# Rotary embedding of two attentions: block copies and VectorE in place of TensorE permutation matmuls

## The reference

```python
def rope(x, pos):
    half = HEAD_DIM // 2
    inv = ROPE_THETA ** (-jnp.arange(half) / half)
    ang = pos[:, None] * inv[None, :]
    cos, sin = jnp.cos(ang)[None, :, None, :], jnp.sin(ang)[None, :, None, :]
    x1, x2 = x[..., :half], x[..., half:]
    return jnp.concatenate([x1 * cos - x2 * sin, x2 * cos + x1 * sin], axis=-1)

q = rope(q.reshape(b, s, N_HEADS, dh), pos)
ks = rope(ks.reshape(b, s, g_n, dh), pos)      # selected keys
kw = rope(kw.reshape(b, s, g_n, dh), pos)      # window keys
kc_c = compress(kc, cmp_pos[0], ...)           # blocks of 32 tokens + position bias, gelu MLP
```

## Time and profile before

| | |
|---|---|
| time, median of 3 runs | 1591.09 us (1590.78 to 1593.4) |
| the profiled execution's own time | 1591.71 us |
| its span, first to last instruction | 1589.9 us |
| TensorE busy | 1548.1 us, 97% |
| VectorE busy | 1179.4 us, 74% |
| ScalarE busy | 974.5 us, 61% |
| HBM read | 243.09 MB |
| granted TensorE clock, mean | 0.994 |

### The profile page before, as it was taken

How to read it: one execution, slowest core, us unless ns; L and a number is a source line. 1 busy time by engine, 2 the same in 40 slices (tenths; PEclk the granted TensorE clock), 3 DMA queues, 4 the chain that set the end, 5 groups by cost and what they waited for, 6 DMA issues and landing times.

```text
span 1589.9 us, 31250 instructions
## 1 busy us (share of the span) xinstructions
PE 1548.1 (97%) x13494; PEld 1460.2 (92%) x13494; DVE 1179.4 (74%) x1665; ACT 974.5 (61%) x1440; POOL 2.8 (0%) x10
## 2 busy tenths in 40 slices
PE   8999999999999999999999999989999998999998
PEld 7999999999989999999999887958999987799997
DVE  6899657777668799467777566866888677688864
ACT  7676864665547777665656451476777555677753
POOL 0000000000000000000000000000000000000000
PEclk9999999999999999999999999989999999999999
DMA  7523145555544321354655544501655543165551
GB/s 280 177 91 107 56 151 190 200 196 180 196 160 161 133 101 62 111 208 160 212 182 189 186 166 154 177 6 54 212 186 186 189 163 133 53 206 189 186 189 53
DMA packets 35849, 246.15 MB, mean 155 GB/s; under 512 B 4096, under 2 KB 4480, under 8 KB 6656
## 3 DMA queue, kind: packets, MB, share of 16 engines
q1 hardware_dynamic: 35712, 244.15, 44.5%
HBM read 243.09 MB, written 1.05 MB: 154 GB/s over the span
## 4 chain that ended last, share of the span: by engine, by line
PE 81%; DVE 12%; ACT 4%; DMA 1%; issue 1%; SPq 0%; DVEq 0%; ACTq 0%
PE PS L407 80%; DVE WL L1932 3%; DVE SB L1941 2%; DVE SB L1932 2%; ACT SB L1222 1%; ACT WH L1225 1%; DVE SA L1932 1%; DMA RAW<-w_in 1%; PE PS L410 1%; ACT SB L1225 1%; DVE SB L2200 1%; DVE SB L1936 0%; ACT SB L1798 0%; DVE SA L1941 0%; DVE SA L2102 0%
## 5 line engine op out<-in xcount | busy, mean ns | idle before, releaser
L407 PE MATMUL PS<-XH,WH 128*128 128x256 f32 (+1 forms) x2536 | 715.9, 282 | 11.5 <-DVE WL L1932 4.4
L407 PE MATMUL PS<-XL,WH 128*128 128x256 f32 (+1 forms) x2536 | 712.9, 281 | 0.0
L407 PE MATMUL PS<-XH,WL 128*128 128x256 f32 (+1 forms) x2536 | 712.6, 281 | 0.0
L1225 ACT CAST WH<-RAW 128x2048 fp32r<-128x2048 f32 (+1 forms) x229 | 427.0, 1865 | 369.9 <-PE PS L407 343.5
L1932 DVE TENSOR_TENSOR WL<-RAW,WH 128x2048 fp32r<-128x2048 f32 (+1 forms) x229 | 511.3, 2234 | 136.4 <-ACT WH L1225 132.3
L407 PEld LDWEIGHTS PS<-XH,WH 128*128 128x128 f32 (+1 forms) x2536 | 477.4, 188 | 18.6 <-issue 6.6
L407 PEld LDWEIGHTS PS<-XL,WH 128*128 128x128 f32 (+1 forms) x2536 | 475.4, 187 | 3.1 <-issue 2.4
L407 PEld LDWEIGHTS PS<-XH,WL 128*128 128x128 f32 (+1 forms) x2536 | 474.9, 187 | 0.4
L407 PE MATMUL PS<-INHL,WH 128*128 128x512 f32 (+1 forms) x1216 | 334.5, 344 | 1.2 <-DVE INHL L1932 1.2
L407 PE MATMUL PS<-INHL,WL 128*128 128x256 f32 x960 | 270.0, 281 | 0.0
L407 PEld LDWEIGHTS PS<-INHL,WH 128*128 128x128 f32 x1216 | 210.0, 188 | 29.2 <-ACT INHL L1225 1.5
(11 more groups left out here) (145 smaller groups left out, 1307.6 us busy)
## 6 DMA issues: line engine op xcount, KB each, us to landing
RAW<-w_in SPq DMA_DIRECT2D x51, 1024.0 KB, 4.9
RAW<-w_up SPq DMA_DIRECT2D x44, 1024.0 KB, 4.8
RAW<-f_in SPq DMA_DIRECT2D x44, 1024.0 KB, 4.9
RAW<-w_down SPq DMA_DIRECT2D x22, 1024.0 KB, 4.9
RAW<-f_out SPq DMA_DIRECT2D x22, 1024.0 KB, 4.8
RAW<-a_w_in SPq DMA_DIRECT2D x10, 1024.0 KB, 4.9
RAW<-w_out SPq DMA_DIRECT2D x8, 1024.0 KB, 4.8
RAW<-w_bdn SPq DMA_DIRECT2D x4, 1024.0 KB, 4.8
```

The lines of the kernel that those rows point to most:

```text
L407: return e.matmul(out, l, r, start=start, stop=stop, skip_group_check=True)
L1225: e.copy(out, x).then_inc(*A.up(*key, of=of))
```

## The change

TensorE no longer takes part in the rotation of queries and keys, nor in doubling the compressor's inputs.

- Queries: VectorE multiplies the projection from PSUM by the sines into `SN` and by the cosines into `RAWQ` (512 columns each). ScalarE copies `SN` to `TN` in four copies of 32 partitions, each block to its neighbour's place. VectorE subtracts `TN` from `RAWQ`. (Before, the sines' sign was that of the target half; taken at the source half, it calls for a subtraction.)
- Keys of the first attention: the same, two heads at a time; the result goes to one half of the partitions, and ScalarE copies it to the other half. Keys of the second attention: the same with 256 columns.
- Compressor: VectorE adds the bias to `kc_raw`, `vc_raw` in SBUF, and takes the source half's partitions for both target halves; the bias lies in a second, turned copy.
- `CD` and its two loads are gone. ScalarE's ten copies from PSUM to SBUF (`k_raw`, `q_raw`) are gone.
- The compressed keys are still rotated with `ROT`.
- Waits: scores wait for a whole query chunk and for both key projections.

```diff
+            def turned_halves(st, name, i, width=512):          # ScalarE
+                w.wait_ge(*V[name + " in", st, i])
+                if name == "q":
+                    waits(*([V["rope q", st, i - 2]] if i > 1 else [V["rope k", st, 0 if st == "s" else i]]))
+                for j in range(4):
+                    cp(TN[i % 2][QUART[j], 0:width], SN[i % 2][QUART[j ^ 1], 0:width], name + " turned", st, i)
...
+                def both_halves(n):
+                    w.wait_ge(*V["rope k", st, n])
+                    for h in range(2):
+                        cp(KKv[HALF[1 - h], h:4:2, n], KKv[HALF[h], h:4:2, n], "rope k", st, n)
...
-                k_raw(0)
-                k_raw(1)
+                chunk()
+                chunk()
                 hidden(0, 0)
                 hidden(0, 1)
+                turned_halves(st, "k", 0)
                 hidden(1, 0)
-                chunk()
+                turned_halves(st, "k", 1)
+                chunk()
+                both_halves(0)
                 hidden(1, 1)
+                both_halves(1)
                 tables("exp_and_others")
-                for c in range(4):
+                chunk()
+                w.wait_ge(*P["ps", st, "glT"])
+                act(gl, v3(ps[st, "glT"][:, 0:96], 2), ACT.Exp, "gl exp", scale=-1.0, of=ps.out(st, "glT"))
+                for c in range(3):
                     chunk()
-                    w.wait_ge(*P["ps", st, "q", c, 0])
-                    cp(RAWQ[:, c * 512:c * 512 + 512], ps[st, "q", c, 0][:, :], "q raw", st, c, of=ps.out(st, "q", c, 0))
+                    turned_halves(st, "q", c)
...
+                turned_halves(st, "q", 3)
                 for u in range(16 + 3):
...
+            def rope_in(st, name, i, x, out, cos, sin, of):     # VectorE
+                if name == "q":
+                    waits(*([A["q turned", st, i - 2], V["rope q", st, i - 2]] if i > 1 else
+                            [A["k turned", st, 0 if st == "s" else i]] if i == 0 or st == "n" else []))
+                n = x.shape[-1] // 256
+                x, sn = v3(x, n), v3(SN[i % 2][:, 0:256 * n], n)
+                tt(sn, x, sin.unsqueeze(1).to_broadcast([128, n, 256]), ALU.mult, name + " in", st, i, of=of)
+                tt(v3(out, n), x, cos.unsqueeze(1).to_broadcast([128, n, 256]), ALU.mult, name + " in", st, i, of=of)
+            def q_out(st, c):
+                s = slice(c * 512, c * 512 + 512)
+                waits(A["q turned", st, c], V["q in", st, c])
+                tt(Q[:, s], RAWQ[:, s], TN[c % 2], ALU.subtract, "rope q", st, c)
...
-                rope_q(st, 1)
-                chunk()
-                rope_q(st, 2)
+                q_out(st, 1)
+                chunk()
+                q_in(st, 2)
+                q_in(st, 3)
+                q_out(st, 2)
...
-                    if u == 1:
-                        rope_q(st, 3)
+                    if u == 0:
+                        q_out(st, 3)
...
                     if t_ < 3:                                  # second attention, VectorE's loop
-                        rope_q(st, t_ + 1)
+                        q_out(st, t_ + 1)
+                    if t_ < 2:
+                        q_in(st, t_ + 2)
```

More of the change, by code:

```diff
@@ L902, in ffn @@
                 down(st, nxt)
[L904 to L914, removed]
             def nsa():
                 st = "n"
[L919 to L926, removed]
                 def hidden(n, hf):
@@ L1041, in scores @@
                     wd, g = 128 * (j + 1), t_ // 2
-                    w.wait_ge(*V["rope q", st, t_])
-                    w.wait_ge(*V["rope k", 0, g])
-                    w.wait_ge(*V["rope k", 1, g])
+                    w.wait_ge(*V["rope q", st, t_ // 2])
+                    for n in range(2):
+                        w.wait_ge(*V["rope k", st, n])
+                        w.wait_ge(*A["rope k", st, n])
                     for r in range(2):
@@ L1893, in swa @@
                     if t_ < 2:
-                        q_raw(t_ + 2)
+                        chunk()
+                        turned_halves(st, "q", t_ + 2)
                     if t_ >= 3:
@@ L2605, in hidden_turn, with k_in, k_out @@
                        of=ps.out(st, "hidT", n))
-                def keys(n):
-                    for g in range(4):
-                        if n or g:
-                            w.wait_ge(*V["rope k", n if g else 0, g - 1 if g else 3])
-                        rope_k((st, "rope k", n, g), KK[:, g * 512 + n * 256:g * 512 + n * 256 + 256], g, "rope k", n, g)
+                def k_in(n):
+                    waits(P["ps", st, "k", n, 0], V["angles", st])
+                    rope_in(st, "k", n, ps[st, "k", n, 0][:, :], KU[n], COSr, SINr, ps.out(st, "k", n, 0))
+                def k_out(n):
+                    waits(A["k turned", st, n], V["k in", st, n])
+                    for h in range(2):
+                        tt(KKv[HALF[h], h:4:2, n], v3(KU[n], 2)[HALF[h]], v3(TN[n], 2)[HALF[h]], ALU.subtract, "rope k", st, n)
                 w.wait_ge(*V["angles", st])
@@ L2746, in swa @@
                 turn_rs(st, 1.0)
-                waits(V["angles", st])
-                for g in range(2):
-                    rope_k((st, "rope k", g), KK[:, g * 256:g * 256 + 256], g, "rope ks", g)
+                waits(V["angles", st], A["kv"])
+                rope_in(st, "k", 0, kv[:, 0:256], KU[0][:, 0:256], COSr, SINr, None)
+                waits(A["k turned", st, 0], V["k in", st, 0])
+                for h in range(2):
+                    tt(KK[HALF[h], h * 256:h * 256 + 256], KU[0][HALF[h], 0:256], TN[0][HALF[h], 0:256], ALU.subtract, "rope k", st, 0)
+                q_in(st, 0)
                 chunk()
-                w.wait_ge(*V["rope ks", 1])
-                rope_q(st, 0)
+                q_in(st, 1)
+                q_out(st, 0)
                 V.note("fs", st)
@@ L2944, in constants @@
     put("ROT", rot)
-    cd = np.concatenate([(s == (64 * g + (p % 64 + r) % 64)[None, :]) for r in (0, 32) for g in range(2)], axis=1)
     inv = f(10000.0) ** (-np.arange(32, dtype=f) / f(32))
```

126 lines of the change are left out of this document (44 added, 82 removed).

## The result

The kernel after takes 1595.58 us at the median (1592.57 to 1597.88) against 1592.88 us for the kernel before, timed beside it: ratio 1.0017, 95% interval 1.001 to 1.0025. It is slower by about 2.7 us where 16 us less were forecast. Its profiled execution took 1592.95 us, with a span of 1591.2 us and a mean granted clock of 0.990.

A forecast was written before the change was run, and what follows sets the result against it. TensorE was taken to bound the kernel; 12.7 us off the first attention (10.7 + 2.55 - 0.6) and 3.3 off the second made 16.0, so 1591.1 us would become 1575.1, range 1569.5 to 1582.

The forecast's parts named there:

- What bounds the kernel: Whole kernel: TensorE, busy 97% of the span; work taken off it is worth its time unless something else stands ready.
- (d): Rival, ScalarE's queue: exchanges delay the next weights' cast in 8 query chunks; at 1.7 us per copy, 1599 us; chance 0.03.
- (e): Rival: the first attention's late chains reach the loop and the saving is waited for; within 3 us of before; chance 0.05.
- TensorE: what goes: Both attentions: 44 plain f32 matmuls of 256 columns leave TensorE, 19.8 us of its work.
- Up to the query projections: First attention: compressor inputs 3.5 us, first keys' rotation 3.6 and 0.9 of the second keys' come off.
- The copies: ScalarE's exchange of halves: four 32x512 copies from SBUF to SBUF, 0.62 us each, 2.5 us.
- (b): Rival: copies between blocks of 32 partitions take 1.0 us each, costing 7 to 8 us, 1583 us; chance 0.09.
- (a): Rival: TensorE's clock falls in the new gaps, 1.7 us per fall, one or two falls, 1577 to 1578.5 us; chance 0.19.
- From T on: First attention after T, the last query chunk's end: 2.55 us come off, 0.6 lost; compressed scores' queries ready at T + 8.5.
- The second attention: First scores 0.55 us late after a wait of 3.8, VectorE then 3.0 us faster; 3.3 us gained in all.

The follow-up runs named there:

- b_wide: The kernel before with PR 32 unused columns wider, so XL and all later tiles lie 128 bytes up: 1603.59 us against 1591.9, ratio 1.0072.
- a_moved: The kernel after with PR back at 836 columns and the turned biases in their own tile behind all others: 1583.27 us, ratio to before 0.9945.
- a_w32_b: Second timing, word for word, of a_w32: ratio to the kernel before 0.9936.
- s_only: The kernel before with the change in the second attention alone, no tile moved: 1589.62 us against 1593.3, ratio 0.9968.
- a_w32: The kernel after with PR 32 columns wider still, so XL and later tiles lie 256 bytes above their old place: 1583.19 us, ratio to before 0.9951.
- a_moved_fill: a_moved with 17 added matmuls whose result nobody reads, in three gaps of TensorE: 1582.3 us, ratio to the kernel before 0.994.
- b_w16: The kernel before with PR 16 unused columns wider, so XL and all later tiles lie 64 bytes up: ratio to before 1.0018.

## Why the prediction was wrong

**What bounds the kernel: right, and read too narrowly.** "Work taken off TensorE is worth its time" held. But an engine at 97% of the span is as exposed to its pace as to its work, and the forecast took the pace of everything it didn't list as fixed. The step that failed is the unwritten one: the parameter tile's 32 new columns were priced at nothing. Their row would have been the projections, 2536 x 3 matmuls; they cost 4.2 ns on each three, 10.7 us by the count, and the matmuls on `INHL` cost 1.5 more; b_wide measured 11.5 us for both. The forecast's range of 12.5 us didn't hold it, nor did any rival: (d) and (e) looked for a loss in queues beside the change. Rival (e), "within 3 us of before", gives the right number for the wrong reason: by luck, since the gain didn't vanish in late chains but was paid for elsewhere.

**TensorE: what goes, right.** 88 records fewer, and the waits of 0.92 and 0.81 us of the earlier trace rows are gone.

**Up to the query projections, right to 0.6 us.** In a_moved the first query chunk starts 39.49 us into the attention instead of 46.92: 7.4 us gained, forecast 3.5 + 3.6 + 0.9 = 8.0. TensorE waits for it 3.14 us (3.54 in the kernel after, 4.08 in a_w32_b), forecast 2.5. The chain named was the right one, but its load took longer than the 4.8 us of the earlier trace rows: from issue to landing 5.3 us in a_moved, 5.7 in the kernel after, 6.2 in a_w32_b. Of the kernel after, SyncE's issue and ScalarE's cast, which waits for the load:

```profile
975.84 0.80 SPq L2838 DMA_DIRECT2D RAW<-a_w_in  x2
...
972.79 2.54 ACT L1186 COPY SA<-SB 32x512 f32<-32x512 f32 x4
981.53 1.90 ACT L1186 CAST WH<-RAW 128x2048 fp32r<-128x2048 f32 x1 [6.20 <-DMA RAW<-a_w_in]
```

**The copies, right.** Four of 32x512 take 2.54 us, forecast 2.5. So (b) and (d), which rest on dearer copies, fall.

**The first attention's clock, a rival that came true beside the forecast.** (a) gave 1.7 us for a fall; the one at the first query chunk costs 1.5. The forecast left it out and gave it a chance of 0.19; it came in five profiles of five. The row that spoke against it, an idle 2.0 us at 1.00, was of a gap shorter than both new ones, and it was one execution's: behind that same wait the clock fell in 8 of the 17 profiles.

**From T on, wrong.** Forecast +1.95 us, in a_moved -1.7. The compressed scores wait 1.02 us where 0.4 was forecast (they start at T + 9.3, not T + 8.5), and the low clock from there to the second value projection costs 3.2 us. The first is a term mis-sized by 0.6; the second had no term, and it is the one whose cause is open.

**The second attention, right as a sum.** 0.63 late (forecast 0.55), a wait of 3.8 (3.8), 3.7 us gained (3.3), and s_only is 3.7 us faster by its medians, 5.1 by its ratio (3.2 to 7.0). Inside it two errors cancel: a fall of the clock behind the gap, and two old falls that went.

**The account.** 16.0 forecast, less 11.5 for the place of `XL`, 1.5 for the clock at the first query chunk, 3.2 for that at the compressed scores and 1.3 for the two longer waits (those of a_moved), and 0.4 more in the second attention: -1.1, against -2.7 measured. The 1.6 us left over are not placed. The clock and the waits are read from a_moved's profiled execution, which was 2.6 us faster than its median.

## What to carry to other kernels

A diff that makes a tile longer moves all the tiles behind it. If one of them is an operand of the matmuls that bound the kernel, time the old kernel with that padding alone before anything is said of the change itself; here it cost 11.5 us and hid a gain of 8.6. In the trace it shows as fewer matmuls in a stretch of the same length that is fully busy at the full clock. And where a change leaves a bound TensorE idle for 3 us ahead of dense work, count the clock's fall behind it too, or put work there: the two together, a_w32 with matmuls in the gaps, gave 1580.42 us, 0.85% below the kernel before. What the filling adds to that (3.8 us by the medians here, 1.0 in a_moved_fill) isn't told apart from nothing, and in the second attention the fall came back later.

## What the runs showed that was not expected

- The pace of f32 matmuls of 256 columns depends on where their moving operand lies in the partition: 353.8 ns for three at the old place of `XL` and 256 bytes above it, 358.0 at 128 bytes above, 359 with `XH` and `XL` both 128 bytes up (300 us / 835 and 836).
- The steps within the three are not equal and shift between stages (in b_w16: 115.1, 115.9, 119.0 ns between 280 and 405 us, 118.7, 117.0, 117.5 between 1400 and 1500). The "110 ns" of the expectations comes from starts rounded to 10 ns, which at 350 ns for three always round alike.
- The matmuls on `INHL` have slow places too: 350.0 ns for its pair of 512 and 256 columns at 64 bytes up (b_w16), 346.7 or 346.8 in all the others that were read.
- After 3.1 to 4.1 us of idle time TensorE was granted the lower clock for 3.3 to 6.1 us of the work behind it in each of five profiles at two places, and matmuls into a free bank kept it at 1.00 there in both profiles that had them; in the second attention it then fell at turn 1. But it also fell within dense stretches, in some executions and not in others.
- Two copies of 64x512 within SBUF took 1.26 us on ScalarE and four of 32x512 2.54: the cost goes by the columns, not by the partitions. Nothing is saved between neighbours: 24 ns lie between them, where most of ScalarE's back-to-back instructions on all 128 partitions overlap by some 96.
